# A two-block transformer on one core: constant products in TensorE's waits, new orders at the joints of stages, rotary and modulation work cut into smaller steps

## The reference

```
x = x + 0.5 * swiglu(rms_norm(x, g1), w_gate, w_up, w_down)          # ffn1, 2816 wide
h = rms_norm(x, mix_norm); a, g, q, k, v = split(h @ w_in)
x = x + concat([conv_module(a, g), diff_attention(q, k, v)]) @ w_out # mixer
x = x + 0.5 * swiglu(rms_norm(x, g2), ...)                           # ffn2
```

## Time and profile before

| | us |
|---|---|
| median of 3 runs (3065.72 to 3066.39) | 3065.81 |
| the profiled execution | 3076.46 |
| its span, first to last instruction | 3074.7 |
| TensorE busy (matmuls, 22556) | 3029.0 |
| DVE busy | 2182.8 |
| ACT busy | 1615.9 |
| POOL busy | 265.1 |

### The profile page before, as it was taken

How to read it: one execution, slowest core, us unless ns; L and a number is a source line. 1 busy time by engine, 2 the same in 40 slices (tenths; PEclk the granted TensorE clock), 3 DMA queues, 4 the chain that set the end, 5 groups by cost and what they waited for, 6 DMA issues and landing times.

```text
span 3074.7 us, 53305 instructions
## 1 busy us (share of the span) xinstructions
PE 3029.0 (99%) x22556; PEld 2857.8 (93%) x22556; DVE 2182.8 (71%) x3452; ACT 1615.9 (53%) x2398; POOL 265.1 (9%) x241
## 2 busy tenths in 40 slices
PE   8999999999999999999999999999999999999999
PEld 8998999999999999999999998879999999999887
DVE  6877787876787656899555557766669975555676
ACT  5565654565644455556544445456445554444454
POOL 0010001010001001820000000000156000000000
PEclk9999999999999999999999999999999999999999
DMA  7762577774377544457856667645445687666663
GB/s 254 259 248 98 192 274 257 274 265 165 115 251 277 174 144 176 165 179 289 294 202 216 217 213 240 206 183 181 163 169 175 233 297 239 218 218 213 221 236 124
DMA packets 153549, 654.61 MB, mean 213 GB/s; under 512 B 10364, under 2 KB 77504, under 8 KB 78816
## 3 DMA queue, kind: packets, MB, share of 16 engines
q1 hardware_dynamic: 96720, 584.09, 53.9%
q10 hardware_dynamic: 56176, 65.66, 6.4%
q0 software_dynamic: 416, 1.45, 0.1%
HBM read 616.55 MB, written 34.61 MB: 212 GB/s over the span
## 4 chain that ended last, share of the span: by engine, by line
PE 88%; DVE 8%; ACT 2%; DMA 1%; issue 1%; ACTq 0%; POOL 0%; DVEq 0%
PE ps L604 18%; PE ps L606 18%; PE ps L605 18%; PE ps L609 9%; PE ps L610 9%; PE ps L611 9%; DVE w_lo L1575 2%; PE ps L1045 2%; PE ps L781 2%; ACT w_hi L1115 1%; DMA raw<-in_ffn_gu 1%; DVE raw L1570 1%; PE ps L676 0%; DVE at L1717 0%; PE ps L1016 0%
## 5 line engine op out<-in xcount | busy, mean ns | idle before, releaser
L1575 DVE TENSOR_TENSOR w_lo<-raw,w_hi 128x1024 fp32r<-128x1024 f32 x932 | 1138.2, 1228 | 609.8 <-ACT w_hi L1115 608.9
L1115 ACT ACTIVATE w_hi<-raw 128x1024 fp32r<-128x1024 f32 x1000 | 1050.8, 1055 | 696.7 <-PE ps L606 419.8
L604 PE MATMUL ps<-h_hi,w_hi 128*128 128x256 f32 x4240 | 1191.2, 281 | 15.4 <-DVE h_lo L1593 10.7
L605 PE MATMUL ps<-h_lo,w_hi 128*128 128x256 f32 x4240 | 1181.7, 279 | 0.0
L606 PE MATMUL ps<-h_hi,w_lo 128*128 128x256 f32 x4240 | 1181.5, 279 | 0.0
L604 PEld LDWEIGHTS ps<-h_hi,w_hi 128*128 128x128 f32 x4240 | 798.2, 188 | 21.7 <-issue 16.9
L606 PEld LDWEIGHTS ps<-h_hi,w_lo 128*128 128x128 f32 x4240 | 803.8, 190 | 0.0
L605 PEld LDWEIGHTS ps<-h_lo,w_hi 128*128 128x128 f32 x4240 | 798.1, 188 | 2.8 <-issue 0.2
L609 PE MATMUL ps<-w_hi,at 128*128 128x512 f32 x1024 | 398.5, 389 | 3.1 <-DVE at L2120 3.1
L611 PE MATMUL ps<-w_hi,at 128*128 128x512 f32 x1024 | 398.4, 389 | 0.0
L610 PE MATMUL ps<-w_lo,at 128*128 128x512 f32 x1024 | 398.3, 389 | 0.0
(11 more groups left out here) (284 smaller groups left out, 3239.6 us busy)
## 6 DMA issues: line engine op xcount, KB each, us to landing
raw<-in_peer_u SPq DMA_DIRECT2D x128, 1024.0 KB, 4.8
raw<-in_peer_v SPq DMA_DIRECT2D x128, 1024.0 KB, 4.8
raw<-in_ffn_gu SPq DMA_DIRECT2D x87, 1024.0 KB, 5.0
raw<-in_ada_w SPq DMA_DIRECT2D x48, 1024.0 KB, 5.3
raw<-in_ffn_down SPq DMA_DIRECT2D x44, 1024.0 KB, 5.0
gates<-at ACTq DMA_DIRECT2D x32, 1024.0 KB, 4.7
at<-gates ACTq DMA_DIRECT2D x24, 1024.0 KB, 6.0
raw<-in_w_in SPq DMA_DIRECT2D x16, 1024.0 KB, 4.8
```

Source lines behind the costliest of these rows:

```text
L604: e.matmul(o, lhs[0], rhs[0], start=start, stop=False)
L605: e.matmul(o, lhs[0], rhs[1], start=False, stop=False)
L1115: e.activation(whi[:, u % NPAIR, :], raw(k, half), ACT.Copy).then_inc(hi_done.hit(u), 1)
L1575: e.tensor_tensor(wlo[:, m % NPAIR, :], raw(k, half), whi[:, m % NPAIR, :].bitcast(FP), ALU.subtract).then_inc(w_lo_dve.hit(m), 1)
```

## The change

It does this, in the order of the diff:
- the second half of an ada piece changes places with the unit of weights behind it in `halves`;
- `stir` multiplies ones by ones (fp32 128x128) into a bank that the next matmul overwrites: 28 at the start, 2 before and 5 behind the scale row of retention and of both peer stages, 1 and 3 at that of sgu;
- `project_pairs` and `project_rows` do the two products of h_hi when that is there, and the one of h_lo after it; banks are taken ahead of the scale row;
- in sgu's output projection outputs 0 and 1 are done together, four blocks of one and four of the other, with the weights in that order; z tiles are issued at inputs 4 and 8; `out_after` gives output 0 as complete with output 1;
- `ready_root` is called in retention's output projection too, and at the end of a peer stage after the copies and the splitting of weights, which are no longer ahead of the last step;
- the last u pair ahead of the sweep is handled on ACT and DVE after the first products;
- `norm` splits its unit of weights in two halves, one ahead of the tiles, one behind tile 2;
- the rotary work is cut in two functions, called at f = 4, 5, 7 and 8, the sines at f = 6 and 9, the copy at f = 10.

```diff
@@ -240,6 +240,9 @@
             lo_key[n + half] = (lo, lo_count[lo])
+for i in range(1, len(halves) - 1):
+    if halves[i][1:3] == (1, "ada") and halves[i + 1][1:3] == (0, "v"):
+        halves[i], halves[i + 1] = halves[i + 1], halves[i]
 w_lo_dve = signal("w_lo_done_dve", lambda n: lo_key[n][1])
@@ -420,6 +423,8 @@
+    if key == "sgu_out":
+        m = max(m, 1)
     if (m + 1) * K % BLK == 0:
@@ -610,6 +615,11 @@
+    def stir(o, count):
+        for _ in range(count):
+            e.matmul(o[:, 0:128], ones, ones, start=True, stop=True)
     def weights(n):
@@ -643,25 +653,35 @@
                 c = slice(k * 128, (k + 1) * 128)
+                w.wait_ge(h_hi, h_hi(q, k))
+                for half in range(2):
+                    wh, wl = weights(unit[key, 2 * (n + z) + half])
+                    s = slice(half * T, (half + 1) * T)
+                    e.matmul(o[:, s], wh[:, c], hh_[:, k, :], start=k == 0 and half == 0, stop=False, skip_group_check=True)
+                    e.matmul(o[:, s], wl[:, c], hh_[:, k, :], start=False, stop=False, skip_group_check=True)
+                w.wait_ge(h_lo, h_lo(q, k))
                 for half in range(2):
...
                     wh, wl = weights(g)
-                    w.wait_ge(h_lo, h_lo(q, k))
-                    t = loose(o[:, half * T:(half + 1) * T], (wh[:, c], wl[:, c]), h_part(k), k == 0 and half == 0, k == KT - 1)
+                    t = e.matmul(o[:, half * T:(half + 1) * T], wh[:, c], hl_[:, k, :], start=False, stop=k == KT - 1, skip_group_check=True)
                     if k == KT - 1:
...
-    def project_rows(q, key, n, r, name, between=None):
-        b = [take(banks, (*name, tt)) for tt in range(2)]
+    def project_rows(q, key, n, r, name, between=None, b=None):
+        if b is None:
+            b = [take(banks, (*name, tt)) for tt in range(2)]
         for u in range(4):
...
                     kk = 2 * u + k
-                    c = slice(k * 512, (k + 1) * 512)
+                    c, s = slice(k * 512, (k + 1) * 512), slice(tt * 128, (tt + 1) * 128)
+                    w.wait_ge(h_hi, h_hi(q, kk))
+                    e.matmul(b[tt], hh_[:, kk, s], wh[:, c], start=kk == 0, stop=False)
+                    e.matmul(b[tt], hh_[:, kk, s], wl[:, c], start=False, stop=False)
                     w.wait_ge(h_lo, h_lo(q, kk))
-                    t = triple(b[tt], h_part(kk, slice(tt * 128, (tt + 1) * 128)), (wh[:, c], wl[:, c]), kk == 0, kk == KT - 1)
+                    t = e.matmul(b[tt], hl_[:, kk, s], wh[:, c], start=False, stop=kk == KT - 1)
                 if tt == 0 and u == 3:
@@ -690,11 +710,14 @@
-    def out_project(q, key, K, rhs, ready, c=None, last=True, first={}):
+    def out_project(q, key, K, rhs, ready, c=None, last=True, first={}, joint=1):
         n, blk = unit[key, 0], 0
-        for m in range(KT):
-            b = take(banks, ("out", q, m))
-            for i in range(K):
+        for ms in [range(joint)] + [(m,) for m in range(joint, KT)]:
+            bs = [take(banks, ("out", q, m)) for m in ms]
+            step = K if len(ms) == 1 else BLK // 2
+            for m, i in ((m, i + d) for i in range(0, K, step) for m in ms for d in range(step)):
+                b = bs[m - ms[0]]
                 if blk % BLK == 0:
@@ -707,7 +730,7 @@
                     n += 1
-                elif i == K - 1:
+                elif i == K - 1 and K % BLK > 0:
                     t.then_inc(down_done.hit(c, m), 1)
@@ -903,8 +926,11 @@
         q = 6
+        outs = [take(banks, ("rq", n)) for n in range(2)]
+        stir(outs[0], 2)
         scale_row(q)
-        project_pairs(q, "ret_qk", 0, [take(banks, ("rq", n)) for n in range(2)])
+        stir(outs[0], 5)
+        project_pairs(q, "ret_qk", 0, outs)
         for n in range(2, 8):
@@ -957,9 +983,12 @@
         q = 8
+        outs = [take(banks, ("sv", 0, tt)) for tt in range(2)]
+        stir(outs[0], 1)
         scale_row(q)
+        stir(outs[0], 3)
         for c in range(6):
-            project_rows(q, "sgu_v", c, 6 + c, ("sv", c))
+            project_rows(q, "sgu_v", c, 6 + c, ("sv", c), b=outs if c == 0 else None)
             if c == 1:
@@ -983,12 +1012,15 @@
         out_project(q + 1, "sgu_out", 24, lambda c: (z_hi[:, c, :].rearrange("p (a b) -> p a b", a=2), z_lo[:, :, c * 128:(c + 1) * 128]),
-                    lambda c: (z_lo_done, z_lo_done(c)), first={5: lambda: z_tiles(10), 10: lambda: z_tiles(11)})
+                    lambda c: (z_lo_done, z_lo_done(c)), first={4: lambda: z_tiles(10), 8: lambda: z_tiles(11)}, joint=2)
...
         ub, gb, qb = Banks([0, 1]), Banks([2, 3, 4, 5, 6]), Banks([4, 5, 6])
+        outs = [take(qb, ("pq", l, n)) for n in range(2)]
+        stir(outs[0], 2)
         scale_row(q)
+        stir(outs[0], 5)
@@ -1087,6 +1119,7 @@
     w.wait_ge(consts, 1)
+    stir(psum[6], 28)
     for l in range(L):
@@ -1151,8 +1184,8 @@
                 w_hi_upto(unit[key, 0] + (m + 1) * K // BLK + NPAIR)
-            if m == 1 and q in (6, 9):
-                ready_root((6, 9).index(q))
+            if m == 1 and q in (6, 7, 9):
+                ready_root((6, 7, 9).index(q))
             if gains is not None:
@@ -1192,8 +1225,8 @@
                 e.activation(lam[:, 4:8], bank["lam",][:, 0:4], ACT.Exp).then_inc(lam_exp.hit(), 1)
-            if c == 3 and f in (5, 7):
-                n = (f - 5) // 2
+            if c == 3 and f in (6, 9):
+                n = (f - 6) // 3
                 w.wait_ge(sin_ready, sin_ready(n))
@@ -1493,7 +1526,7 @@
         g_store(15)
-        for n in range(NTOP + NBUILD, NPAIRS):
+        for n in range(NTOP + NBUILD, NPAIRS - 1):
             u_pair(n)
@@ -1507,18 +1540,19 @@
         products(0)
+        u_pair(NPAIRS - 1)
         for n in range(64):
...
                 products(n + 1)
-            for e2 in range(2):
-                w_hi_upto(unit[("peer_v", l), 2 * n + e2] + NPAIR)
+                for e2 in range(2):
+                    w_hi_upto(unit[("peer_v", l), 2 * n + e2] + NPAIR)
             if n + NPAIRS < 64:
                 u_pair(n + NPAIRS)
-        ready_root(2 + l)
         for k in range(3):
...
         w_hi_upto(unit[("peer_v", l), 127] + 1 + NPAIR)
+        ready_root(3 + l)
         for m in range(KT):
@@ -1575,6 +1609,19 @@
+    def w_lo_part(u, part):
+        if split[0] > u:
+            return
+        k, half, lo, m = halves[split[1]]
+        assert lo == "v" and m == u and split[0] == u
+        c = slice(part * UNIT // 2, (part + 1) * UNIT // 2)
+        w.wait_ge(hi_done, hi_done(u))
+        t = e.tensor_tensor(wlo[:, u % NPAIR, c], raw(k, half)[:, c], whi[:, u % NPAIR, c].bitcast(FP), ALU.subtract)
+        if part == 1:
+            t.then_inc(w_lo_dve.hit(u), 1)
+            split[0], split[1] = u + 1, split[1] + 1
     def step(t):
@@ -1614,7 +1661,9 @@
         token_scale(q)
-        w_lo_upto(first + NPAIR)
+        if dst is None:
+            w_lo_upto(first + NPAIR - 1)
+            w_lo_part(first + NPAIR - 1, 0)
@@ -1632,6 +1681,8 @@
                 lower(m - 1)
+            if m == 2:
+                w_lo_part(first + NPAIR - 1, 1)
         if dst is None:
@@ -1655,26 +1706,29 @@
-    def rotary_angle(n):
+    MAGIC = 12582912.0
+    def rotary_turns(n):
         if n == 0:
...
             step(e.tensor_scalar(ang, tp, col("inv_freq"), None, ALU.mult))
+        stepped()
+        if n == 1:
+            w.wait_ge(sin_done, sin_done(0))
+        step(e.tensor_scalar(w0, ang, 1.0 / (2 * math.pi), (0.0, 0.25)[n], ALU.mult, ALU.add))
+        stepped()
+        step(e.tensor_scalar(nr, w0, MAGIC, None, ALU.add))
+        stepped()
+        step(e.tensor_scalar(nr, nr, -MAGIC, None, ALU.add))
+    def rotary_rest(n):
         C1 = 6.28125
...
         c3 = float(np.float32(2 * math.pi - C1 - c2))
-        MAGIC = 12582912.0
-        off, bias_v = ((0.0, 0.0), (0.25, math.pi / 2))[n]
-        stepped()
-        if n == 1:
-            w.wait_ge(sin_done, sin_done(0))
-        step(e.tensor_scalar(w0, ang, 1.0 / (2 * math.pi), off, ALU.mult, ALU.add))
-        stepped()
-        step(e.tensor_scalar(nr, w0, MAGIC, None, ALU.add))
-        stepped()
-        step(e.tensor_scalar(nr, nr, -MAGIC, None, ALU.add))
+        bias_v = (0.0, math.pi / 2)[n]
         src = ang
@@ -1701,9 +1755,11 @@
                 bias_tiles()
-            if c == 3 and f in (4, 6):
-                rotary_angle((f - 4) // 2)
-            if c == 3 and f == 8:
+            if c == 3 and f in (4, 7):
+                rotary_turns((f - 4) // 3)
+            if c == 3 and f in (5, 8):
+                rotary_rest((f - 5) // 3)
+            if c == 3 and f == 10:
                 w.wait_ge(sin_done, sin_done(1))
@@ -2120,15 +2176,17 @@
         products(0)
+        pair(("peer_u", l), NPAIRS - 1)
         for n in range(64):
...
                 products(n + 1)
-            for e2 in range(2):
-                w_lo_upto(unit[("peer_v", l), 2 * n + e2] + NPAIR)
+                for e2 in range(2):
```

(16 more changed lines are left out.)

## The result

| kernel | median us | runs | from | to |
|---|---|---|---|---|
| before | 3066.10 | 4 | 3065.72 | 3067.41 |
| after | 3121.11 | 4 | 3112.85 | 3123.61 |

The ratio after to before is 1.017, 95% interval 1.0153 to 1.0186: slower by 55 us, where 3051.8 and a range of 3042 to 3063 were forecast. The profiled execution of after has a span of 3119.1 us.

What follows compares the result with a forecast made beforehand. TensorE, busy 3029.0 of 3074.7 us, was taken as the bound, leaving idle time, slow clock and matmul pitch to win. Terms summed to -14.0, taken off 3065.8: 3051.8 us, range 3042 to 3063.

Steps and rivals of the forecast that it cites:

- ada and rotary order: Ada blocks and last ffn: swapping halves brings the first w_lo forward, rotary work is spread; -0.5 us, bounds -3 and +2.
- Rival (c): Ffns: raw buffer released some 3 us later, new w_lo waits in the middle ones; +10 us, 3076; chance 0.07.
- pitch: Time between matmuls, 112.6 or 117.1 ns, drawn anew where waits move; -2 us, bounds -11 and +8.
- start: First matmuls: products of ones keep the clock, half of the 2.4 us held back; -1.2 us, bounds 0 and -2.4.
- entry of retention: 1009 to 1016 us: products of h_hi start earlier, clock expected to hold; -1.4 us, bounds +0.9 and -2.0.
- entry of the first peer stage: 1216 to 1228 us: table load hidden under earlier matmuls, clock kept; -4.2 us, bounds -1.3 and -4.9.
- entry of the second peer stage: 2255 to 2266 us: clock kept, root already loaded in time; -2.5 us, bounds +0.9 and -3.2.
- both sweeps: Entries at 1497 and 2537 us: first products made earlier, p_lo waits vanish; -3.1 us, bounds 0 and -3.2.
- entry of sgu: 2020 to 2037 us: sums end earlier, h_hi first, clock back sooner; -1.9 us, bounds +1 and -3.2.
- sgu output projection (the new wait): 2189 to 2198 us: TensorE idles 2.0 us more after unit 5 and loses clock; +2.8 us, bounds +0.5 and +4.5.
- Rival (b): Joints: products of constants do not keep the clock; total gain only -4.2 us, 3061.6; chance 0.19.
- Rival (d): Sgu's output projection: the new wait does not come, DVE's update being off the path; 3049; within a shared chance of 0.60.

Runs made afterwards that it cites:

- long hold: Kernel before, DVE's and ACT's orders untouched; SP waits for w_lo of the unit after the next before loading an ada block's raw buffer: 3110.62 us.
- experiment 7: Kernel after without the swap, rows 0 and 1 of sgu's output projection one after the other as before: 3055.61 us, ratio 0.996.

## Why the prediction was wrong

**The failed step is "ada and rotary order".** It said of the swap that it "brings the first w_lo 1.14 us forward, but the second ends when it did", and took -0.5 with a bound of +2. It measured +59 alone and +62 to +64 beside the other edits. I priced the time on DVE, which is the same in both orders, and not the buffer that the moved half holds. The second half does not end when it did, but 4.7 us later, because `w_lo_upto` stops as soon as its unit is done, and what is swapped behind the last unit of a call slides into the next call.

**Rival (c) had the mechanism, at a chance of 0.07 and a third of its size** (+22 us for the swap, which cost 59 to 64). It put the release at some 3 us later; it was 4.7. It took the two middle ffns' lead of about 5 us as a cover that would hold, and priced the loss there as pitch, 19 us. But the hold comes again with every fourth load (6 of the 22 issued from 400 to 500). In 400 to 500 the ring moved 272 GB/s before and 238 after, so a lead is used up and never earned back, and the middle ffns lost 37 us (15.7 to 52.3 in the table), more than the first with 15 and the last with 6. (Against the kernel without the swap, whose pitch in the first ffn was the shorter one, it is 37, 21 and 9.) "It decides when DMA has a backlog" was the wrong test: DMA was less busy (0.65 for 0.76). What was scarce was buffers, as the long hold shows, which keeps a buffer and changes nothing else. "It is wrong if waits for w_lo appear in the middle ffns" was the right one.

**The other terms,** by the same matmuls, in the kernel without the swap:

| step | predicted | measured |
|---|---|---|
| start | -1.2 | -1.0 to -1.5 |
| entry of retention | -1.4 | -0.8 to -1.05 |
| entry of the first peer stage | -4.2 | -4.5 to -4.7 |
| entry of the second peer stage | -2.5 | -2.1 to -2.6 |
| both sweeps | -3.1 | -3.4 to -3.8 |
| entry of sgu | -1.9 | +0.5 to +1.85 |
| sgu output projection (the new wait) | +2.8 | +2.0 to +2.7 |
| sum with -2 for pitch, no order | -13.5 | -10.3 by the medians |

The ranges are over four traces without the swap, against the first trace of before; the projection's is the difference of experiment 7. The first peer entry, the sweeps and the projection came as argued: no table load ahead of rcol, no wait for p_lo, and in the projection a wait of 2.24 us and, behind the sixth unit, a new one of 1.80 us, where 3 and 2 were forecast. (By the Trainium skill, "ScalarE: Activation LUTs", "What ACT_TABLE_LOAD costs", the first peer entry would have won 1.3 us more than my 4.2; it won 0.3 to 0.5 more, and 0.5 is what the clock gives when it is kept for certain and not at 85 of 100.) Rival (b) is out: in after the clock is held at three of four entries. Rival (d) did not occur.

The entry of sgu failed by its sign. I had the first square begin at 2025.3 in the time of before, and it came at 2024.9 (2077.11 less the 52.2 us by which after is late there). I had the sums end at their old time less 0.7, since squares bound them; they end at 2084.3, which is 2.1 us later than their old time. For I let the clock come back, when the transposes now run early and at full clock and leave 2.9 us of nothing before the first sum: the clock falls there, and is at 0.50 from 2078 to 2088, through sums, scale row and the first matmuls. The sums then take 6.7 us, and TensorE bounds them and not the squares. Before, the wait of 1.94 us stood ahead of the transposes and they brought the clock back before the sums.

**The base.** All terms were read from an execution of 3076.46 us and taken off a median of 3065.8. The second trace of before shows that executions differ by 7 us at the same order and nearly the same waits, in the joints' clock and in the pitch of a few stretches, and 18 runs of before on one chip went from 3059 to 3075. A clock term read from one execution has that error; my range was wide enough for it, and it had no part in the miss.

## What to carry to other kernels

When an instruction is moved, ask first what it releases, and not what it takes: with a ring of three buffers and 1 MB loads of 5 us, 1.4 us of longer hold was free and 4.6 us cost 42. Only these two lengths were held alone; where between them the loss begins was not measured. Where work is emitted by calls with a stopping rule, look up in which call a swapped item lands, since the wait at the head of the next call comes with it. A lead that covers one late load does not cover one in every four.

## What the runs showed of the hardware

The pitch of the same matmuls is 112.6 or 117.1 ns for whole stretches at a granted clock of 1.00, and can differ between two executions of one program (427 and 437 matmuls in 2200 to 2250). Products of ones of 128 columns kept the granted clock at 1.00 over joints with about 2 us without other work, in 20 of 21 cases. A wait of 2.9 us behind transposes lost it for 10 us; a wait of 1.94 us lost it in one execution of before and not in the other. The down projections' loads took 6.1 us from issue to landing, by the median, where they had taken 5.0, while DMA moved less. In after, releases came in pairs and loads were issued close together (at 423.12 and 424.26, behind the block shown above). Between 100 and 1000 us its loads issued less than 1.6 us from a neighbour landed after 6.0 us (78 loads, median), the others after 5.0 (95). Each table load of before takes 1.28 us on ACT and begins 0.02 us behind the instruction ahead of it; in 23 of the 44 cases the next begins 0.01 to 0.03 us behind the load.
